# Byte offsets of the moving operands in on-chip memory: FFN activations at byte 32 of 128, token sums at 32, 96 and 64

## The chip, the cores and the metric

The kernel runs on one core of a Trainium2 chip. The metric is the device time of one execution in microseconds (us). Every product is a TensorE matmul: a tile of weights is loaded into the array (LDWEIGHTS, shown as engine PEld) and then the activations stream past it as the moving operand (MATMUL, shown as PE). VectorE is DVE, ScalarE is ACT, GpSimd is POOL, SyncE is SP.

## The reference, cut to what matters

Two blocks of two layers each work on 512 tokens of width 1024 in float32. Six feed-forward networks (FFN) of hidden width 2816 lie in them, and between them projections and attention. What is computed in each FFN:

```python
def swiglu(x, w_gate, w_up, w_down):
    return (jax.nn.silu(x @ w_gate) * (x @ w_up)) @ w_down

def swiglu_ffn(h, w_gate_up, w_down):
    g, u = jnp.split(h @ w_gate_up, 2, axis=-1)
    return (jax.nn.silu(g) * u) @ w_down
```

## The kernel before

**Three products for one.** The kernel keeps a float32 value as a high and a low part of type fp32r. A tile product is three matmuls: high weights by high activations, low weights by high activations, high weights by low activations. Each of them has its own weight load of 128x128. The function `piece` (lines 749 to 751), the functions `chunk_high` and `chunk_low` (757, 758, 761), the early part of the down projection (982 to 984) and the output projections (1388 to 1390) do this with 512 tokens as the moving operand; `product` (899 to 901) does it with 256.

**An FFN has three parts.** First 8 plain pieces of gate and up (24 matmuls of 512 tokens each). Then 9 pairs of hidden chunks: a pair makes four quadrants (gate and up, first and second half of the tokens) from seven products instead of eight, with sums of weights and sums of token halves. A product is 24 matmuls of 256 tokens, a pair 168. Last the down projection, 22 hidden chunks by 8 output chunks, 528 matmuls of 512 tokens or their halves.

**Which tiles the seven products of a pair read** (lines 911 to 926): products 0, 3 and 5 stream the normalised activations HH and HL; product 1 streams the token sum TH[0] and TL[0], product 2 TH[1], product 4 TH[2], product 6 TH[3]. The weights come from the slots that `part_slots` names: (1, 2, 3, 0, 8, 9, 10) for products 0 to 6, or (2, 3, 0, 1, 8, 9, 10) in the two FFNs of the second block.

**Where the tiles lie.** `region` hands out bytes of each partition one after the other; tile sizes are multiples of 32 bytes. The first byte is 16512, a multiple of 128. HH, HL and weight slots 0 to 3 begin at byte 0 of their 128. Behind Y come small tables with 9920 bytes in all, so that the arena `ar` of 88 KB begins at 139072, which is byte 64 of its 128. In the arena lie the hidden activations HIDL and HIDH, the four token sums, the projections, the latents CH and CL, the attention output OH and OL and the normalised memory NH and NL, all at offsets of whole KB, and the weight slots 4 to 8; slots 9 and 10 lie outside at byte 0. A slot holds 8 KB: low weights in the first 4 KB, high weights in the second. Each 128x128 tile in it is 512 bytes further, and a chunk of activations is 1 or 2 KB further, so that all tiles of one buffer have the same byte of their 128. In the table "moving" and "weights" are these bytes:

| matmuls | moving | weights | columns |
|---|---|---|---|
| HH by slots 0 to 3, 9 | 0 | 0 | 512 and 256 |
| HH by slots 4 to 7 | 0 | 64 | 512 |
| HIDH, CH, OH by slots 0 to 3 | 64 | 0 | 512 (a few HIDH: 256) |
| NH by slots 0 to 3 | 64 | 0 | 256 |
| products 1, 2 and 6 | 64 | 0 | 256 |
| product 4 (slot 8) | 64 | 64 | 256 |

**Order around it.** SP issues the weight loads (`load`, `part`), POOL adds weight sums for the pairs (lines 658, 663, 669) or splits plain pieces (629, 631), ACT makes high parts (1697 in pairs, 1718 in the down projection), DVE low parts (2240, 2316), and PE waits for them by semaphores. The order on each engine is written out by hand.

Of the kernel before, what the change touches and what calls it, by code (L numbers as in the profile page):

```python
# [131 lines left out]
def program(nc, A, trips):  # L132
# [5 lines left out]
    def region(n):  # L138
        o = at[0]
        at[0] += n  # L140
        assert at[0] <= nc.sbuf_usable_end, at[0]
        return o

    def sb(name, shape, dt=F32, offset=None):
        n = int(np.prod(shape[1:])) * (2 if dt == BF16 else 4)
        o = region(-(-n // 32) * 32) if offset is None else offset
        return nc.alloc_sbuf_tensor_at(name, list(shape), dt, offset=o)

    KB = 1024
# [4 lines left out]
    slot_at = [region(8 * KB) for _ in range(RING)]  # L154
# [4 lines left out]
    SQo = region(4 * KB)  # L159
# [4 lines left out]
    Yo = region(16 * KB)  # L164
# [11 lines left out]
    stat = sb("stat", [P, 8, 4])  # L176
    top8 = sb("top8", [P, QB, 8])
    WIT = sb("WIT", [P, QB, IDXH], offset=RYo)
    ar = region(88 * KB)
    slot_at += [ar + 72 * KB, ar + 80 * KB, ar + 28 * KB, ar + 36 * KB, ar + 64 * KB, SQo, Yo + 8 * KB]  # L180
    raw = [sb(f"raw{j}", [P, TILES * P], offset=o) for j, o in enumerate(slot_at)]
    WL = [sb(f"WL{j}", [P, TILES * P], F32R, offset=o) for j, o in enumerate(slot_at)]
    WH = [sb(f"WH{j}", [P, TILES * P], F32R, offset=o + 4 * KB) for j, o in enumerate(slot_at)]
# [1 line left out]
    HIDL = sb("HIDL", [P, KF, S], F32R, offset=ar)  # L185
    HIDH = sb("HIDH", [P, KF, S], F32R, offset=ar + KF * 2 * KB)
    BF = sb("BF", [P, KD, S], offset=ar + 8 * KB)
    sum_at = [ar + 48 * KB, ar + 56 * KB, ar + 72 * KB, ar + 80 * KB]
    TF = [sb(f"TF{i}", [P, HALF_K, HALF], offset=o) for i, o in enumerate(sum_at)]
    TL = [sb(f"TL{i}", [P, HALF_K, HALF], F32R, offset=o) for i, o in enumerate(sum_at)]  # L190
    TH = [sb(f"TH{i}", [P, HALF_K, HALF], F32R, offset=o + 4 * KB) for i, o in enumerate(sum_at)]
# [1367 lines left out]
    def _(act):  # L1559
# [443 lines left out]
        for kind in ("dsa", "dil"):  # L2003
# [17 lines left out]
            if kind == "dsa":  # L2021
                act.wait_ge(vt_ready, n.full(vt_ready))
                act.activation(WIT[:], index_weight_bank.rearrange("p (b c) -> p b c", c=P)[:, :, 0:IDXH],
                               ACT.Copy, scale=float(IDXH ** -0.5 * HD ** -0.5)).then_inc(vt_done, 1)
# [25 lines left out]
    def _(dve):  # L2050
# [567 lines left out]
        def logit(i):  # L2618
# [5 lines left out]
            if h == 0:  # L2624
                ins = dve.tensor_scalar(score[b][:], got, WIT[:, b, h:h + 1], None, ALU.mult)
            else:
                ins = dve.scalar_tensor_tensor(out=score[b][:], in0=got, scalar=WIT[:, b, h:h + 1],
                                               in1=score[b][:], op0=ALU.mult, op1=ALU.add)
# [330 lines left out]
def build(nc, arrays, trips):  # L2959
    A = {k: nc.dram_tensor(f"in_{k}", v.shape, mybir.dt.from_np(v.dtype), kind="ExternalInput").ap() for k, v in arrays.items()}  # L2960
    A["out"] = nc.dram_tensor("out_0", (KD, P, S), F32, kind="ExternalOutput").ap()
    program(nc, A, trips)
# [14 lines left out]
```

## Time and profile before

| what | value |
|---|---|
| median of 3 runs | 3335.26 us (3335.03 to 3341.03) |
| span of the profiled execution | 3337.3 us |
| PE busy | 3229.6 us (97%) |
| PEld busy | 2729.8 us (82%) |
| DVE, ACT, POOL busy | 2059.6, 1359.2, 1345.4 us |
| mean granted TensorE clock | 0.993 |

The profiled execution is 2.0 us longer than the median. The time of a matmul in a row of the timeline is its latency (0.28 or 0.39 us), and neighbours overlap. What counts is the distance from the start of one to the start of the next: it is read here as the start of the first matmul of a group of 24 and the start of the first one of the next group, divided by 24.

### The profile page before, as it was taken

The numbers are of one execution on the slowest core, as the hardware profiler recorded it, in microseconds if no ns is written. First come the engines' busy times: TensorE is split into PE (matmuls) and PEld (weight loads), VectorE is DVE, ScalarE is ACT, GpSimd is POOL, SyncE is SP. The second block draws the span as 40 slices with busy tenths as digits, with TensorE's granted clock in tenths as the row PEclk, the third lists the DMA queues.
The fourth block names the chain that finished last, engine by engine and source line by source line (L and its number), as shares of the span: only waits on it lengthen the run. The fifth ranks groups of instructions, "written<-read, shape, count | busy, mean of one in ns | idle before, by whom it ended". The sixth has DMA issues, their size and how long they took to land.

```text
span 3337.3 us, 51827 instructions
## 1 busy us (share of the span) xinstructions
PE 3229.6 (97%) x19480; PEld 2729.8 (82%) x19487; DVE 2059.6 (62%) x2673; ACT 1359.2 (41%) x2335; POOL 1345.4 (40%) x643
## 2 busy tenths in 40 slices
PE   8999999999999999999999999998999999999998
PEld 7998775789877899877579987765789987879986
DVE  7774444586647876354477765678477734477753
ACT  5553225344435445322444543324435521254542
POOL 6320562554116541065164404656553107635300
PEclk9999999999999999999999999999999999999999
DMA  4543221255332454322035533221145433215532
GB/s 156 159 143 104 90 87 32 70 152 151 114 123 83 138 160 120 105 83 87 19 99 153 153 117 108 101 68 34 51 135 166 123 103 108 82 57 146 168 104 95
DMA packets 99977, 362.59 MB, mean 109 GB/s; under 512 B 11088, under 2 KB 11344, under 8 KB 99536
## 3 DMA queue, kind: packets, MB, share of 16 engines
q1 hardware_dynamic: 88704, 320.90, 29.4%
q0 software_dynamic: 7776, 28.32, 5.1%
q10 hardware_dynamic: 3312, 10.86, 0.9%
q8 instruction: 122, 2.00, 0.2%
q14 instruction: 63, 0.52, 0.0%
HBM read 355.84 MB, written 4.19 MB: 108 GB/s over the span
## 4 chain that ended last, share of the span: by engine, by line
PE 73%; DVE 10%; issue 6%; ACT 4%; POOL 3%; DMA 3%; DVEq 0%; ACTq 0%; POOLq 0%; SPq 0%
PE psC L749 4%; PE psC L751 4%; PE psC L750 4%; PE psA L749 4%; PE psA L751 4%; PE psA L750 4%; PE psD L899 2%; PE psD L900 2%; PE psD L901 2%; PE psB L899 2%; PE psB L900 2%; PE psB L901 2%; DVE WL L2240 2%; DMA Y<-in_ws 2%; PE psB L984 2%
## 5 line engine op out<-in xcount | busy, mean ns | idle before, releaser
L629 POOL TENSOR_TENSOR WH<-raw,scalars 128x1024 fp32r<-128x1024 f32 (+1 forms) x194 | 377.8, 1948 | 1206.5 <-DMA raw<-in_w 1143.3
L2240 DVE TENSOR_TENSOR WL<-raw,WH 128x1024 fp32r<-128x1024 f32 x324 | 447.9, 1385 | 70.5 <-POOL raw L663 39.8
L631 POOL TENSOR_TENSOR WL<-raw,WH 128x1024 fp32r<-128x1024 f32 (+1 forms) x194 | 471.2, 2429 | 15.2
L1697 ACT ACTIVATE WH<-raw 128x1024 fp32r<-128x1024 f32 x324 | 340.4, 1053 | 48.9 <-DMA raw<-in_ws 37.2
L2316 DVE TENSOR_TENSOR WL<-raw,WH 128x1024 fp32r<-128x1024 f32 (+1 forms) x144 | 163.1, 1135 | 307.4 <-ACT WH L1718 305.8
L658 POOL TENSOR_TENSOR raw<-raw,Y 128x1024 f32<-128x1024 f32 x54 | 133.4, 2471 | 509.6 <-DMA raw<-in_ws 509.6
L1718 ACT ACTIVATE WH<-raw 128x1024 fp32r<-128x1024 f32 (+1 forms) x144 | 141.9, 989 | 375.7 <-DMA raw<-in_w 375.7
L749 PE MATMUL psA<-HH,WH 128*128 128x512 f32 x560 | 230.0, 411 | 0.0
L751 PE MATMUL psA<-HL,WH 128*128 128x512 f32 x560 | 218.5, 390 | 0.0
L750 PE MATMUL psA<-HH,WL 128*128 128x512 f32 x560 | 218.3, 390 | 0.0
L899 PE MATMUL psD<-TH,WH 128*128 128x256 f32 x720 | 202.0, 281 | 6.2 <-DVE psC L2287 2.7
L900 PE MATMUL psD<-TH,WL 128*128 128x256 f32 x720 | 200.5, 279 | 0.0
L901 PE MATMUL psD<-TL,WH 128*128 128x256 f32 x720 | 200.3, 278 | 0.0
L749 PE MATMUL psC<-HIDH,WH 128*128 128x512 f32 x484 | 191.8, 396 | 3.5 <-DVE WL L2316 3.5
L750 PE MATMUL psC<-HIDH,WL 128*128 128x512 f32 x484 | 191.4, 396 | 0.0
L751 PE MATMUL psC<-HIDL,WH 128*128 128x512 f32 x484 | 191.4, 395 | 0.0
L899 PE MATMUL psB<-TH,WH 128*128 128x256 f32 x576 | 161.9, 281 | 5.1 <-ACT psB L1734 5.1
L669 POOL TENSOR_TENSOR raw<-raw,raw 128x1024 f32<-128x1024 f32 x54 | 142.8, 2645 | 47.3 <-PE psB L901 27.5
L900 PE MATMUL psB<-TH,WL 128*128 128x256 f32 x576 | 160.6, 279 | 0.0
L901 PE MATMUL psB<-TL,WH 128*128 128x256 f32 x576 | 160.4, 278 | 0.0
L899 PEld LDWEIGHTS psD<-TH,WH 128*128 128x128 f32 x720 | 135.9, 189 | 8.3 <-DVE psC L2287 3.5
L663 POOL TENSOR_TENSOR raw<-raw,raw 128x1024 f32<-128x1024 f32 x54 | 134.0, 2482 | 13.4 <-POOL raw L658 11.6
(540 smaller groups left out, 9631.1 us busy)
## 6 DMA issues: line engine op xcount, KB each, us to landing
raw<-in_w SPq DMA_DIRECT2D x338, 512.0 KB, 3.5
raw<-in_ws SPq DMA_DIRECT2D x216, 512.0 KB, 3.6
Y<-in_ws SPq DMA_DIRECT2D x54, 512.0 KB, 4.7
raw<-in_ws POOLq DMA_DIRECT2D x54, 512.0 KB, 5.4
X<-in_x ACTq DMA_DIRECT2D x4, 512.0 KB, 9.5
NRAW<-in_mem ACTq DMA_DIRECT2D x2, 1024.0 KB, 7.2
out<-Y SPq DMA_DIRECT2D x8, 256.0 KB, 2.1
POSI<-in_pos ACTq DMA_DIRECT2D x4, 256.0 KB, 2.6
```

The lines of the kernel that those rows point to most:

```text
L629: pool.tensor_tensor(WH[j][:, 0:w], raw[j][:, 0:w], zero[:, 0:1].broadcast_to([P, w]), ALU.subtract).then_inc(w_hi, 1)
L631: pool.tensor_tensor(WL[j][:, 0:w], raw[j][:, 0:w], WH[j][:, 0:w], ALU.subtract).then_inc(w_split, 1)
L669: pool.tensor_tensor(raw[slots[5]][:], raw[slots[2]][:], raw[slots[3]][:], ALU.add).then_inc(sum_ready, 1)
L749: pe.matmul(out, WH[slot][:, w], hi[:, t], start=start and t == 0, stop=False)
L750: pe.matmul(out, WL[slot][:, w], hi[:, t], start=False, stop=False)
L751: mm = pe.matmul(out, WH[slot][:, w], lo[:, t], start=False, stop=stop and t == tiles - 1)
L899: pe.matmul(o, WH[slot][:, w], hi[:, k], start=start and half == 0 and k == 0, stop=False, skip_group_check=True)
L900: pe.matmul(o, WL[slot][:, w], hi[:, k], start=False, stop=False, skip_group_check=True)
L901: mm = pe.matmul(o, WH[slot][:, w], lo[:, k], start=False, stop=half == 1 and k == HALF_K - 1, skip_group_check=True)
L1697: act.activation(WH[slots[i]][:], DX if i == 6 else raw[slots[i]][:], ACT.Copy).then_inc(part_hi, 1)
L2240: dve.tensor_tensor(WL[slots[i]][:], DX if i == 6 else raw[slots[i]][:], WH[slots[i]][:], ALU.subtract).then_inc(part_lo, 1)
L2316: dve.tensor_tensor(WL[j][:, 0:w], raw[j][:, 0:w], WH[j][:, 0:w], ALU.subtract).then_inc(down_lo, 1)
```

## The change

```diff
     WIT = sb("WIT", [P, QB, IDXH], offset=RYo)
+    region(96)
     ar = region(88 * KB)
-    slot_at += [ar + 72 * KB, ar + 80 * KB, ar + 28 * KB, ar + 36 * KB, ar + 64 * KB, SQo, Yo + 8 * KB]
+    slot_at += [ar + 72 * KB, ar + 80 * KB, ar + 28 * KB, ar + 36 * KB, ar + 64 * KB - 160, SQo, Yo + 8 * KB]
...
-    sum_at = [ar + 48 * KB, ar + 56 * KB, ar + 72 * KB, ar + 80 * KB]
+    sum_at = [ar + 48 * KB - 256, ar + 56 * KB - 192, ar + 72 * KB - 96, ar + 80 * KB - 96]
```

The arena moves up by 96 bytes, from byte 64 to byte 32 of its 128. With it move HIDL, HIDH, the projections, CH, CL, OH, OL, NH, NL and the weight slots 4 to 7. The token sums are placed by themselves: TH[0] at byte 32, TH[1] at 96, TH[2] and TH[3] at 64, where the last two were. Slot 8, which holds the weights of product 4, goes from byte 64 to byte 0. No instruction, wait, transfer or size is added, removed or moved.

| matmuls | moving, weights before | after |
|---|---|---|
| HIDH, CH, OH (512 columns), NH (256) | 64, 0 | 32, 0 |
| HH by slots 4 to 7 | 0, 64 | 0, 32 |
| product 1 | 64, 0 | 32, 0 |
| product 2 | 64, 0 | 96, 0 |
| product 4 | 64, 64 | 64, 0 |
| product 6 | 64, 0 | 64, 0 |
| HH by slots 0 to 3, 9 | 0, 0 | 0, 0 |

## Rows read from the trace of the kernel before

**Rows 1.** The page: span, busy time of each engine, TensorE's clock in 40 slices.

```profile
span 3337.3 us, 51827 instructions
PE 3229.6 (97%) x19480; PEld 2729.8 (82%) x19487; DVE 2059.6 (62%) x2673; ACT 1359.2 (41%) x2335; POOL 1345.4 (40%) x643
PEclk9999999999999999999999999999999999999999
```

**Rows 2.** Stretches: two pairs, one disturbed pair, down projection. Busy us (instructions), clock, DMA.

```profile
102.68:122.33 19.65, 19.65 (x171) 19.65 (x169) 14.09 (x18) 9.23 (x15) 8.03 (x4) 1.00 0.57 161
122.33:141.98 19.65, 19.65 (x171) 19.65 (x170) 14.65 (x18) 10.12 (x15) 8.22 (x6) 1.00 0.57 162
1829.90:1850.70 20.80, 19.98 (x170) 19.79 (x169) 15.15 (x19) 9.84 (x14) 9.69 (x5) 1.00 0.52 151
335.00:346.20 11.20, 11.20 (x50) 9.02 (x49) 3.05 (x3) 3.09 (x4) 0.00 (x0) 1.00 0.32 95
```

**Rows 3.** Timeline of PE, first matmul of products 0 to 6, then next pair.

```profile
102.68 0.28 PE L899 MATMUL psC<-HH,WH 128*128 128x256 f32 x1
105.54 0.29 PE L899 MATMUL psC<-TH,WH 128*128 128x256 f32 x1
108.28 0.28 PE L899 MATMUL psD<-TH,WH 128*128 128x256 f32 x1
111.00 0.28 PE L899 MATMUL psC<-HH,WH 128*128 128x256 f32 x1
113.86 0.28 PE L899 MATMUL psD<-TH,WH 128*128 128x256 f32 x1
116.72 0.28 PE L899 MATMUL psD<-HH,WH 128*128 128x256 f32 x1
119.59 0.29 PE L899 MATMUL psD<-TH,WH 128*128 128x256 f32 x1
122.33 0.28 PE L899 MATMUL psA<-HH,WH 128*128 128x256 f32 x1
```

**Rows 4.** Timeline of PE, hidden by slots 0 to 3: firsts of three pieces of 24.

```profile
335.40 0.39 PE L749 MATMUL psC<-HIDH,WH 128*128 128x512 f32 x1
...
341.00 0.39 PE L749 MATMUL psC<-HIDH,WH 128*128 128x512 f32 x1
...
346.60 0.39 PE L749 MATMUL psC<-HIDH,WH 128*128 128x512 f32 x1
```

**Rows 5.** Timeline of PE: HH by slot 1 (2442.36), by slot 6 (2447.80), next piece.

```profile
2442.36 0.39 PE L749 MATMUL psC<-HH,WH 128*128 128x512 f32 x1
...
2447.80 0.39 PE L749 MATMUL psA<-HH,WH 128*128 128x512 f32 x1
...
2453.30 0.39 PE L749 MATMUL psB<-HH,WH 128*128 128x512 f32 x1
```

**Rows 6.** Timeline of PE: attention output OHa, 24 matmuls between its two rows.

```profile
2406.32 0.39 PE L1388 MATMUL psC<-OHa,WH 128*128 128x512 f32 x1
...
2411.93 0.39 PE L1388 MATMUL psC<-OHa,WH 128*128 128x512 f32 x1
```

**Rows 7.** Timeline of PE: normalised memory NH, 24 matmuls between its two rows.

```profile
2258.11 0.28 PE L749 MATMUL psA<-NH,WH 128*128 128x256 f32 x1
...
2260.93 0.28 PE L749 MATMUL psA<-NH,WH 128*128 128x256 f32 x1
```

**Rows 8.** Groups of PE instructions: count | busy us, mean ns | idle before, by whom.

```profile
L749 PE MATMUL psC<-HIDH,WH 128*128 128x512 f32 x484 | 191.8, 396 | 3.5 <-DVE WL L2316 3.5
L982 PE MATMUL psB<-HIDH,WH 128*128 128x512 f32 x264 | 104.4, 396 | 0.0
L982 PE MATMUL psA<-HIDH,WH 128*128 128x512 f32 x264 | 104.4, 395 | 0.0
L749 PE MATMUL psC<-CH,WH 128*128 128x512 f32 x68 | 28.3, 416 | 1.9 <-DVE PROJ L2406 1.9
L1388 PE MATMUL psC<-OHa,WH 128*128 128x512 f32 x64 | 25.4, 397 | 0.0
L1388 PE MATMUL psC<-OHb,WH 128*128 128x512 f32 x32 | 12.8, 399 | 0.0
```

**Rows 9.** Waits: who waited for whom, us in total, times, longest.

```profile
POOL raw L658 <- DMA raw<-in_ws: 509.6, 48, 13.2
ACT WH L1718 <- DMA raw<-in_w: 375.7, 114, 6.3
DVE WL L2316 <- ACT WH L1718: 305.8, 98, 6.0
```

## The prediction

> **What bounds the kernel now.** The page comes first: PE is busy 3229.6 of 3337.3 us, and no other engine passes 62% but the weight loads, which run beside PE [rows 1]. Such a share alone proves little, since a share is a mean, so the second view is the stretches: in an undisturbed pair and in the down projection PE is busy in all of the time, at a granted clock of 1.00, which is the 2.4 GHz level [rows 2]. So the end is set by how quickly one matmul follows another, and the third view is the timeline, read for distances between starts. There the reader is to see that matmuls of one size don't all follow at one distance, and what goes with the difference. In one pair the seven products of 24 matmuls of 256 columns last 2.86, 2.74, 2.72, 2.86, 2.86, 2.87 and 2.74 us [rows 3]. The products that stream HH (0, 3, 5) and product 4 take 2.86: in these four the moving operand and the weights begin at the same byte of their 128. The products whose activations begin at 64 and whose weights at 0 (1, 2, 6) take 2.72 to 2.74. Settled, that is 120 ns for equal bytes (2.86/24 is 119.2; the first few of a product are shorter) and 113 to 114 ns for 64 apart. Product 4 shows that it isn't the tile: it streams a token sum as product 6 does, into the same bank, and costs what HH costs.
>
> With 512 columns it is the other way round. Equal bytes take 5.44/24 = 226.7 ns, HH at 0 with weights at 64 5.50/24 = 229.2 [rows 5], and hidden activations at 64 with weights at 0 5.60/24 = 233.3 [rows 4]; the attention output, in the same position, 5.61/24 = 233.8 [rows 6]. The memory rows, 256 columns, activations at 64 and weights at 0, take 2.82/24 = 117.5 [rows 7], and not 113: the same bytes can settle at two distances, and which one depends on how the stretch is entered. 15 of the 108 products 1 and 2 have 118, 1 of the 54 products 6.
>
> **The change part by part.** Nothing is added or removed; every cost is a count times a change of distance. PE is full where these matmuls lie, so a saved nanosecond is a nanosecond of the end unless a wait takes it.
>
> *Product 4, equal bytes to 64 apart.* It becomes what product 6 is, behind a product that streams HH, as product 6 is. 54 of them (six FFNs, nine pairs): 2.86 to 2.74 is 0.12 us, by the unrounded medians 2.855 and 2.739, so 54 x 0.116 = 6.3 us less. If it settled at 118 always, 2.82 [rows 7], only 54 x 0.03 = 1.6 less. I take 6.3, since only 5 of the 108 products 1 and 6, which also follow HH, are at 118.
>
> *512 columns, activations 64 to 32.* Hidden: 3 x 484 + 6 x 264 = 3036; latents 3 x 68 and attention output 3 x 96 are 492 more [rows 8]; 3528 together. No row has 32, so it needs bounds. Below: a matmul of 256 columns is 106.7 ns shorter than one of 512 with the same bytes (226.7 against 120), so the best 256-column distance, 113.3, stands for 220.0 with 512; that is 13.3 less than now, 47 us. Above: the hidden matmuls alternate between 231 and 236 ns, and a settled 236 would be 2.7 more, 9.5 us. Of the three positions with 512 columns two lie at 226.7 and 229.2 and only the one that is now left lies at 233.3. I take the mean of those two, 227.9, as nearest: 5.4 x 3528 = 19 us less.
>
> *Products 1 and 2, 64 to 32 and to 96.* 108 products, now at 2.74 and 2.72. Above: what equal bytes cost, 2.86, which is 54 x 0.12 + 54 x 0.14 = 14 us more. Below: by the same amount the other way, 14 less, for nothing in the rows says that 64 is the best place. If the cost rises from 64 towards 0 on both sides, both lose half of it, 7 us; if it falls steadily round the 128 bytes, 32 and 96 lie on opposite sides of 64 and cancel. I take the middle of these, 3.5 more.
>
> *The rest.* HH by slots 4 to 7 (624 matmuls: 3 pieces in four FFNs, 2 in two, 2 at each of five borders, 24 each) goes from 64 apart to 32 apart, between 226.7 and 233.3 where it now has 229.2: 1.6 less to 2.6 more. 264 hidden matmuls of 256 columns and 192 of NH lie between 113 and 120: 1 less to 2 more. Both taken at nothing. The elementwise work is as long on any of the slots, and it has slack: in the down projection ACT waits 376 us for weights to land and DVE 306 us for ACT [rows 9], and both are busy 3.1 of 11.2 us there [rows 2], so PE at 228 ns is still fed. If that cover were gone the 19 us would turn into waits on L2316. In the pairs POOL waits 510 us for transfers [rows 9] and is busy 8 of 19.65 us [rows 2]; but a few pairs already hold PE up (19.98 busy of 20.80 [rows 2]), and in these a faster product 4 gives nothing: at most a quarter of the 6.3.
>
> Sum: -6.3 - 19 + 3.5 = -22 us. The profiled execution is 2.0 us longer than the median, 3335.3, from which I subtract: 3313 us.
>
> The Trainium skill, page "SBUF — State Buffer", section "Who interferes with whom", has a rule that speaks against any effect: TensorE has two independent read ports, one for the moving operand and one for weight loads, and "PE and ACT never wait on anyone". By it the sum would be 0. The trace doesn't agree: product 4 and product 6 differ by 0.12 us in 2.86 though only the bytes differ.
>
> **The rivals.**
> *It does nothing.* The position doesn't matter, and the differences come from the order of the products. Against it: product 4 against 6, and HH by slot 1 against slot 6. 3335 us. The page named above would have it so.
> *32 acts like 64 for the wide ones.* Only product 4 changes: 3335.3 - 6.3 = 3329 us. For it: rows only tell 0 and 64 apart, and a coarse grain is possible; against it, a 64-byte grain would put 32 with 0, which gives the forecast.
> *32 is better than either.* 512 columns fall to 220.0: -47 - 6.3 and 0 to -14 for products 1 and 2, 3268 to 3282 us. For it: in 256 columns the distance of 64 gains 6.7 ns on equal bytes, and nothing says that 226.7 is the floor of the wide ones. The Trainium skill, page "TensorE: Matmul & The Clock Gate", section "Back-to-back issue gap", gives N/2.4 + 2.5 ns, 215.8 for 512 columns; by it the wide ones would save 17.5 x 3528 = 62 us; no row here is that short.
> *Slower: 32 collides longer than 64.* Weight load and moving stream meet for longer: wide ones settle at 236 (+9.5) and products 1 and 2 at the price of equal bytes (+14), less 6.3: +17, 3352 us. For it: 256 columns are now at their best position, and two of the three TH products leave it. It decides once these two terms together pass 6.3 + 6.7 = 13 us.
>
> **How the numbers follow.** A measurement of this kernel can tell about 0.2%, 6.7 us, from no change. Chances: the forecast (wide ones between 226.7 and 230) 0.55; 32 better than either 0.15; 32 acts like 64 0.13; nothing 0.02; slower 0.15. The time is the first one's, 3313. The range leaves out the far half of "better than either" and of "slower": 3280 to 3344. Faster by over 0.2%: 0.55 + 0.15 + a little of the 3329 case, 0.72; within 0.2%: 0.15; slower: 0.13, since some of the slower case stays under 6.7 us.
>
> **What would show it.** Product 4 at 2.74 us; 24 hidden matmuls at 5.44 to 5.50 us instead of 5.60; the same for OHa; products 1 and 2 at 2.68 to 2.80; products 0, 3, 5 and 6 and HH by slots 0 to 3 as before. A down projection with gaps ahead of PE would show that weights had become the bound. The prediction is wrong if 24 hidden matmuls take 5.60 or more, or under 5.35.

## The result

| kernel | median us | against before |
|---|---|---|
| before | 3335.05 (3329.60 to 3341.03, 5 runs) | |
| after | 3347.20 (3344.61 to 3349.41, 5 runs) | 1.0035 (95% interval 1.0025 to 1.0046) |

The change makes the kernel 12 us slower (8 to 15 by the interval). The forecast was 3313 us, with a range from 3280 to 3344. The head of the page of after, to be read beside [rows 1]:

```profile
span 3343.4 us, 51827 instructions
PE 3238.1 (97%) x19480; PEld 2739.2 (82%) x19487; DVE 2060.3 (62%) x2673; ACT 1359.3 (41%) x2335; POOL 1341.2 (40%) x643
PEclk9999999999999999999999999999999999999999
```

The same instructions, PE still full, the clock as before, and no other engine busier by more than 1 us: PE has 8.5 us more, and the weight loads that run beside it 9.4. So the time is looked for again in the distance between matmuls. The timeline of PE in after shows the first matmul of products 0 to 6 of the same pair, and of the next pair (lines are one further down than in [rows 3]):

```profile
102.89 0.28 PE L900 MATMUL psC<-HH,WH 128*128 128x256 f32 x1
105.75 0.28 PE L900 MATMUL psC<-TH,WH 128*128 128x256 f32 x1
108.59 0.28 PE L900 MATMUL psD<-TH,WH 128*128 128x256 f32 x1
111.46 0.28 PE L900 MATMUL psC<-HH,WH 128*128 128x256 f32 x1
114.33 0.28 PE L900 MATMUL psD<-TH,WH 128*128 128x256 f32 x1
117.16 0.28 PE L900 MATMUL psD<-HH,WH 128*128 128x256 f32 x1
120.03 0.29 PE L900 MATMUL psD<-TH,WH 128*128 128x256 f32 x1
122.77 0.28 PE L900 MATMUL psA<-HH,WH 128*128 128x256 f32 x1
```

The pair lasts 19.88 us instead of 19.65. By the medians over all pairs, product 1 went from 2.739 to 2.833 us, product 2 from 2.720 to 2.870, product 4 from 2.855 to 2.822, product 3, whose bytes are as before but which follows product 2, from 2.862 to 2.878; products 0, 5 and 6 are as they were. That is 0.23 us for a pair, 12 us for 54.

The down projection, the 24 matmuls between two firsts as in [rows 4], and below them HH by slot 6 between its two firsts, as in [rows 5]:

```profile
325.30 0.40 PE L750 MATMUL psC<-HIDH,WH 128*128 128x512 f32 x1
...
330.90 0.40 PE L750 MATMUL psC<-HIDH,WH 128*128 128x512 f32 x1
...
2450.17 0.39 PE L750 MATMUL psA<-HH,WH 128*128 128x512 f32 x1
...
2455.76 0.40 PE L750 MATMUL psB<-HH,WH 128*128 128x512 f32 x1
```

The hidden matmuls take 5.60 us for 24, to the hundredth what they took. The 19 us that the forecast expected from them aren't there. HH by slots 4 to 7 went the wrong way, from 5.50 to 5.59 us for 24: 624 matmuls at 233.4 instead of 229.1 ns (both read where they have settled), 2.7 us more. The hidden matmuls of 256 columns, in the timelines of before and then of after, 24 between two rows:

```profile
348.00 0.28 PE L1016 MATMUL psB<-HIDH,WH 128*128 128x256 f32 x1
...
350.73 0.28 PE L1016 MATMUL psC<-HIDH,WH 128*128 128x256 f32 x1
```

```profile
349.80 0.28 PE L1017 MATMUL psB<-HIDH,WH 128*128 128x256 f32 x1
...
352.61 0.28 PE L1017 MATMUL psC<-HIDH,WH 128*128 128x256 f32 x1
```

2.73 to 2.81 us for 24, on 264 matmuls: 0.8 us more. The terms add to 12.4 + 2.7 + 0.8 = 16 us, four more than the medians differ. The two profiled executions differ by only 6.1 us in span. The idle time of PE ahead of the products accounts for about what lies between 16 and 6.1. This is the view of line 900 in after, idle time in us and how often, by what ended it; in before, line 899, the first three of these rows are 14.2, 14.0 and 9.9 us, and all idle time there is 46.8 us against 35.4 here, 11.4 less.

```profile
  issue: 12.5, 17
  DVE WL L2241: 9.5, 16
  ACT psB L1735: 7.3, 12
  DVE psC L2288: 6.1, 8
```

That a slower PE gives the weights more time and so shortens the waits would fit, but one execution of each is too little to show it. Apart from the first two pairs of each FFN, 4 pairs last over 0.5 us longer than the steady one in the profiled execution of before, and none in after.

### The profile page after: what moved, and what is told of

It is laid out like the page before. It is cut to its first block, busy times and chain, and to the rows that moved or that the text cites. A ratio compares the mean times of both kernels' runs of the same rounds, so it can differ in the third digit from the quotient of the medians.

```text
span 3343.4 us, 51827 instructions
## 1 busy us (share of the span) xinstructions
PE 3238.1 (97%) x19480; PEld 2739.2 (82%) x19487; DVE 2060.3 (62%) x2673; ACT 1359.3 (41%) x2335; POOL 1341.2 (40%) x643
## 4 chain that ended last, share of the span: by engine, by line
PE 79%; DVE 9%; issue 5%; ACT 4%; POOL 2%; DMA 1%; DVEq 0%; ACTq 0%; SPq 0%; POOLq 0%
PE psC L750 4%; PE psC L752 4%; PE psC L751 4%; PE psA L750 4%; PE psA L752 4%; PE psA L751 4%; PE psD L902 3%; PE psD L900 3%; PE psD L901 3%; PE psB L900 3%; PE psB L902 3%; PE psB L901 3%; PE psC L902 2%; PE psC L900 2%; PE psC L901 2%
## 5 line engine op out<-in xcount | busy, mean ns | idle before, releaser
L2241 DVE TENSOR_TENSOR WL<-raw,WH 128x1024 fp32r<-128x1024 f32 x324 | 450.3, 1393 | 58.1 <-ACT WH L1698 29.2
```

The costliest lines, as they stand in the source:

```text
L2241: dve.tensor_tensor(WL[slots[i]][:], DX if i == 6 else raw[slots[i]][:], WH[slots[i]][:], ALU.subtract).then_inc(part_lo, 1)
```

## The experiments

Bytes are told from here on modulo 256, for a reason that the third experiment gives. In before the arena begins at 64 of 256, HH and the slots outside the arena at 128. In after the arena is at 160, the four sums at 160, 224, 64 and 64, and slot 8 at 0. "Difference" is the byte of the moving operand less that of the weights, modulo 256.

### The arena alone (e1)

```diff
+    region(96)
     ar = region(88 * KB)
...
-... ar + 64 * KB, SQo, Yo + 8 * KB]
+... ar + 64 * KB - 96, SQo, Yo + 8 * KB]
...
-    sum_at = [ar + 48 * KB, ar + 56 * KB, ar + 72 * KB, ar + 80 * KB]
+    sum_at = [ar + 48 * KB - 96, ar + 56 * KB - 96, ar + 72 * KB - 96, ar + 80 * KB - 96]
```

> Only the arena moves to byte 32 of 128; the four token sums and slot 8 stay at byte 64, as before. The theory (position theory: the distance from one matmul to the next is set by the bytes of moving operand and weights, and for 512 columns 32 costs what 64 costs) expects 24 hidden matmuls at 5.60 us, a steady pair at 19.65 us as before, the hidden matmuls of 256 columns at 118 instead of 113 ns, and a time within 3 us of before. The rival, that the move of the arena itself costs (weights land in slots 4 to 7 at another byte, other engines write to another byte), expects most of the 12 us here.

Measured: 3334.29 us, ratio 1.0001 (0.9988 to 1.0013). 24 hidden matmuls take 5.60 us and the seven products what they took in before, with a steady pair of 19.65. The interval is 4 us either way, and the 3.5 us of the HH pieces and of the narrow hidden matmuls are inside it. The arena's move, with everything that DMA and the other engines write at new bytes, is not what costs the 12 us.

### The two sums alone (e2)

```diff
-    sum_at = [ar + 48 * KB, ar + 56 * KB, ar + 72 * KB, ar + 80 * KB]
+    sum_at = [ar + 48 * KB - 160, ar + 56 * KB - 96, ar + 72 * KB, ar + 80 * KB]
```

> Only the first two token sums move, to bytes 32 and 96; arena, slot 8 and the other sums as before. The position theory expects product 1 to go from 2.74 to 2.83 us and product 2 from 2.72 to 2.87, a steady pair of 19.65 + 0.09 + 0.15 + 0.02 = 19.91 us, over 54 pairs 14 us: about 3349. The rival (move of the arena costs) expects a time within 2 us of before.

Measured: 3348.36 us, ratio 1.0044 (1.0027 to 1.0061), 15 us more, 9 to 20 by the interval: as much as the whole change, as far as the two intervals tell. Products 1 and 2 between their firsts and that of product 3, timeline of PE in this kernel:

```profile
106.04 0.28 PE L899 MATMUL psC<-TH,WH 128*128 128x256 f32 x1
108.87 0.28 PE L899 MATMUL psD<-TH,WH 128*128 128x256 f32 x1
111.74 0.28 PE L899 MATMUL psC<-HH,WH 128*128 128x256 f32 x1
```

2.83 and 2.87 us, as in after. The steady pair is 19.91 us, as expected. These two experiments settle where the 12 us came from: the place of the two sums.

### Slot 8 alone (e3)

```diff
-    ar = region(88 * KB)
-... ar + 64 * KB, SQo, Yo + 8 * KB]
+    ar = region(88 * KB + 128)
+... ar + 64 * KB + 64, SQo, Yo + 8 * KB]
...
-    sum_at = [ar + 48 * KB, ar + 56 * KB, ar + 72 * KB, ar + 80 * KB]
+    sum_at = [ar + 48 * KB, ar + 56 * KB, ar + 72 * KB + 128, ar + 80 * KB + 128]
```

> Slot 8 moves from byte 64 to byte 0, the third and fourth sums move by 128 bytes and so keep byte 64 of 128; the rest as before. Product 4 was 2.86 us before and is 2.82 in the changed kernel (118 ns settled), though product 6, with the same bytes of 128, is 2.74 (113 ns). Three theories. Only bytes of 128 count and product 4 was held at 118 by what ran before it (product 2 at byte 96, then product 3): product 4 at 2.74, product 6 at 2.74, pair 19.53, 6 us less. Bytes of 256 count (moving less weights is 64 of 256 for product 4 in the changed kernel and 192 for product 6): here both are 64 of 256, so both 2.82, pair 19.70, 2 to 3 us more. Something of slot 8 or of the third sum by itself: product 4 2.82, product 6 2.74, pair 19.62, 2 us less.

Measured: 3339.50 us, ratio 1.0019 (1.0008 to 1.0029). Timeline of PE in this kernel, firsts of products 4, 5 and 6 and of the next pair:

```profile
114.50 0.28 PE L899 MATMUL psD<-TH,WH 128*128 128x256 f32 x1
117.33 0.29 PE L899 MATMUL psD<-HH,WH 128*128 128x256 f32 x1
120.22 0.28 PE L899 MATMUL psD<-TH,WH 128*128 128x256 f32 x1
123.05 0.29 PE L899 MATMUL psA<-HH,WH 128*128 128x256 f32 x1
```

Products 4 and 6 both take 2.83 us, in all 54 pairs settled at 118 ns. Product 6 has the same bytes of 128 as in before, where it took 2.74: only its sum has moved by 128. So positions 128 bytes apart aren't the same, and a theory in bytes of 128 is too coarse. Of the three theories put down, bytes of 256 stands. The products that follow 4 and 6 begin some 0.01 to 0.02 us worse (2.883 for products 5 and 0 by the medians), so that the pair is 19.75 and not 19.70.

### The arena at the weights' byte (e4)

```diff
+    region(64)
     ar = region(88 * KB)
...
-... ar + 64 * KB, SQo, Yo + 8 * KB]
+... ar + 64 * KB - 128, SQo, Yo + 8 * KB]
...
-    sum_at = [ar + 48 * KB, ar + 56 * KB, ar + 72 * KB, ar + 80 * KB]
+    sum_at = [ar + 48 * KB - 192, ar + 56 * KB - 192, ar + 72 * KB - 64, ar + 80 * KB - 64]
```

> The arena begins at byte 0, so that the hidden, latent and attention matmuls of 512 columns have equal bytes, as HH by slots 0 to 3; the four sums stay at byte 64 and slot 8 is at byte 0. Position theory: 24 hidden matmuls go from 5.60 to 5.44 us, 3528 x 6.6 ns = 23 us less, hidden matmuls of 256 columns from 113 to 120 (2 us more), HH by slots 4 to 7 from 229 to 227 (1.5 less), product 4 at 2.74 (6 us less) or 2.82 (2 less): 3335 - 29 = 3306 or 3310. If bytes of 256 count, products 1, 2 and 4 are all at 64 of 256 and take 2.82: 10 us worse, 3318. If the wide matmuls' distance comes from the tile (hidden) and not from its byte, 5.60 stays and the time is near 3330.

Measured: 3323.53 us, ratio 0.9961 (0.9940 to 0.9982). Timeline of PE, 24 hidden matmuls, then 24 of HH by slot 6:

```profile
325.47 0.39 PE L750 MATMUL psC<-HIDH,WH 128*128 128x512 f32 x1
...
330.91 0.39 PE L750 MATMUL psC<-HIDH,WH 128*128 128x512 f32 x1
...
2440.70 0.39 PE L750 MATMUL psA<-HH,WH 128*128 128x512 f32 x1
...
2446.14 0.39 PE L750 MATMUL psB<-HH,WH 128*128 128x512 f32 x1
```

5.44 us in both: the gain that the forecast had looked for at byte 32 is there with both operands at 128 of 256. Products 1, 2 and 4 have the difference 64 here and settled at 118 ns in 53, 53 and 54 of 54 pairs (medians 2.831, 2.827, 2.822 us), and product 6, with 192, at 113 in all. That is what bytes of 256 say, and the steady pair is 19.83 us. The time is 5 us above the 3318 of that case; that case stood for 17 us less than before, and the interval allows 6 to 20.

### A map of the differences (e5 and e6)

The first half:

```diff
+    region(160)
     ar = region(88 * KB)
-... ar + 28 * KB, ar + 36 * KB, ar + 64 * KB, SQo, Yo + 8 * KB]
+... ar + 28 * KB + 32, ar + 36 * KB + 64, ar + 64 * KB - 192, SQo, Yo + 8 * KB]
...
-    sum_at = [ar + 48 * KB, ar + 56 * KB, ar + 72 * KB, ar + 80 * KB]
+    sum_at = [ar + 48 * KB - 224, ar + 56 * KB - 192, ar + 72 * KB - 64, ar + 80 * KB - 64]
```

> A map of distances by the byte of the moving operand less the byte of the weights, taken modulo 256. The theory so far: that difference sets the distance, with 0: 120 ns, 192: 113, 64: 118, 32: 118, 96: 120 for 256 columns, and 0: 227, 64: 229, 192: 233, 32: 233 for 512. Here product 1 has 128, product 2 160, product 4 128, product 6 32; hidden 96; HH by slots 4 and 5 160, by slot 6 128, by slot 7 96. If bytes of 128 were what counts, product 1 and product 4 (0 of 128) take 120, product 2 (32) 118, hidden 233 or less. If bytes of 256 count, product 6 is at 118 and the others are open between 113 and 120, the wide ones between 227 and 233.

The second half:

```diff
+    region(32)
-    ar = region(88 * KB)
-    slot_at += [ar + 72 * KB, ar + 80 * KB, ar + 28 * KB, ar + 36 * KB, ...
+    ar = region(88 * KB + 128)
+    slot_at += [ar + 72 * KB, ar + 80 * KB + 64, ar + 28 * KB + 32, ar + 36 * KB + 128, ...
...
-    sum_at = [ar + 48 * KB, ar + 56 * KB, ar + 72 * KB, ar + 80 * KB]
+    sum_at = [ar + 48 * KB, ar + 56 * KB, ar + 72 * KB + 128, ar + 80 * KB + 128]
```

> Second half of the map: products 1 and 2 have the difference 224 of 256, product 4 128, product 6 96; hidden 224; HH by slot 4 32, by slot 5 224, by slot 6 0, by slot 7 160. The theory (difference modulo 256) expects product 4 as in the first half of the map, product 6 at 120, HH by slot 4 at 233 as hidden at 32, HH by slot 6 at 227, and HH by slot 5 at the value of hidden. If a buffer's own address counted and not the difference, HH by slot 4 would differ from hidden at 32.

One execution of each, 3348.5 and 3348.7 us; what counts is the timeline. With the kernels above, and with those of the last section for 256 columns, the settled distances in ns; behind them the bytes of 256 at which each was seen, moving operand by weights:

| difference | 256 columns (a product, us) | bytes | 512 columns | bytes |
|---|---|---|---|---|
| 0 | 120 (2.86) | 128 by 128, 64 by 64 | 226.7 | 128 by 128 |
| 32 | 117 to 118 (2.83) | 160 by 128 | 233 | 160 by 128, 128 by 96 |
| 64 | 118 (2.82 to 2.83) | 64 by 0, 192 by 128 | 229 | 128 by 64 |
| 96 | 120 (2.87 to 2.88) | 224 by 128 | 233 | 224 by 128, 128 by 32 |
| 128 | 119 (2.85) | 0 by 128, 160 by 32, 224 by 96 | 233 | 128 by 0 |
| 160 | 117 (2.82) | 32 by 128 | 234 | 128 by 224 |
| 192 | 113 (2.72 to 2.74), or 118 (2.82) | 64 by 128, 192 by 0; 128 by 192 | 233 | 64 by 128 |
| 224 | 118 (2.84) | 96 by 128 | 233 | 96 by 128, 128 by 160 |

For 512 columns the differences 0, 64, 128, 160 and 192 were each seen at one pair of bytes alone, so that there the difference and the bytes themselves are not told apart.

With a slot moved to the moving operand's byte, its matmuls fall to 227: HH by slot 6 in the second half (difference 0) and in the first half (128), each 24 matmuls up to the row that follows:

```profile
53.32 0.39 PE L750 MATMUL psB<-HH,WH 128*128 128x512 f32 x1
...
58.77 1.02 PE L770 MATMUL psD<-cf 128*128 128x512 f32 x2
```

```profile
53.25 0.40 PE L750 MATMUL psB<-HH,WH 128*128 128x512 f32 x1
...
58.84 1.02 PE L770 MATMUL psD<-cf 128*128 128x512 f32 x2
```

5.45 against 5.59 us. For 512 columns one difference is good (0), one is fair (64), and the other six are alike. For 256 columns one is good (192) and the other seven lie between 117 and 120. Both expectations held where they named a number, to about 1 ns.

### Every product at its best difference (e7 and e8)

```diff
+    region(64)
     SQo = region(4 * KB)
...
-... ar + 64 * KB, SQo, Yo + 8 * KB]
+... ar + 72 * KB, SQo, Yo + 8 * KB]
...
-    sum_at = [ar + 48 * KB, ar + 56 * KB, ar + 72 * KB, ar + 80 * KB]
+    sum_at = [ar + 48 * KB - 64, ar + 56 * KB - 64, ar + 64 * KB - 64, ar + 80 * KB]
```

> Every wide matmul of the arena at difference 0 and products 1, 2, 4, 5 and 6 at 192 of 256 (SQ, T and Y move by 64 bytes, so slots 9 and 10 and the arena with them; the third sum and slot 8 change places). The theory expects products 4 and 5 at 2.74 us, products 1, 2 and 6 as before, a pair of 19.65 - 0.12 - 0.13 = 19.40 us or 14 us less over 54 pairs, 24 hidden matmuls at 5.44 us (23 us less), hidden of 256 columns at 120 (2 more), HH by slots 4 to 7 at 227 (1.5 less): 3333 - 36 = 3297. The rival is that POOL's chain of sums, which now ends ahead of PE in a pair, takes over at 19.65 us: then 3311. A second rival: with differences 64 instead of 192 for product 5, because the weights and not the activations were moved, product 5 takes 2.82 and the sum is 5 us smaller.

Measured: 3316.14 us, ratio 0.9939 (0.9924 to 0.9954). Hidden at 5.44 us and product 4 at 2.74 as expected, but products 5 and 6 take 2.82 and 2.83, though their difference is 192. The pair is 19.59 us and not 19.40, which is 10 us over 54 pairs; with these, 3308 would have been expected instead of 3297, and the measured time is 8 us above that. What the two products have in common is that their weights begin at 192, in slots 9 and 10.

The next kernel keeps those two slots as they were:

```diff
+    region(64)
     ar = region(88 * KB)
...
-... ar + 64 * KB, SQo, Yo + 8 * KB]
+... ar + 80 * KB, SQo, Yo + 8 * KB]
...
-    sum_at = [ar + 48 * KB, ar + 56 * KB, ar + 72 * KB, ar + 80 * KB]
+    sum_at = [ar + 48 * KB - 64, ar + 56 * KB - 64, ar + 64 * KB - 64, ar + 72 * KB - 64]
```

> The arena begins at byte 0 of 128 (128 of 256), as the weights; all four sums begin at 64 of 256 and slot 8 at 128, the pairing that gave 113 ns in every run so far; slots 9 and 10 as before. Bytes of moving operand and weights are now (64, 128) of 256 for products 1, 2, 4, 6 and (128, 128) for all the rest. Expected: products 1, 2, 4, 6 at 2.72 to 2.74 us, products 0, 3, 5 at 2.86, a steady pair of 19.65 - 0.12 = 19.53 us, against 19.59 with e7; hidden at 5.44 us; 3527 matmuls x 6.6 ns = 23 us less, 6 less from product 4, 1.5 less from HH by slots 4 to 7, 2 more from hidden of 256 columns: 3334 - 28 = 3306. The rival (the chain of sums and splits, which already held up some pairs, takes what product 4 gives): pairs with gaps ahead of PE, and 3312.

Measured: 3315.24 us, ratio 0.9941 (0.9928 to 0.9953): 17 us under the before measured beside it (16 to 24 us by the interval), where after lies 12 above its own, with nothing changed but addresses. Timeline of PE in this kernel, firsts of the products 3 to 6 and of the next pair, in a pair without waits:

```profile
760.43 0.28 PE L900 MATMUL psA<-HH,WH 128*128 128x256 f32 x1
763.29 0.29 PE L900 MATMUL psB<-TH,WH 128*128 128x256 f32 x1
766.03 0.28 PE L900 MATMUL psB<-HH,WH 128*128 128x256 f32 x1
768.89 0.29 PE L900 MATMUL psB<-TH,WH 128*128 128x256 f32 x1
771.63 0.28 PE L900 MATMUL psC<-HH,WH 128*128 128x256 f32 x1
```

All steady distances are what was expected, the pair at 19.52 us. The time is 9 us above 3306, and the 28 us less that were expected lie outside the interval. The idle time of PE ahead of line 900 in this kernel (its profiled execution is the longest of its six, 3323 us):

```profile
  DVE WL L2241: 19.4, 37
  issue: 14.9, 20
  ACT psB L1735: 10.6, 15
  DVE psC L2288: 9.8, 11
  ACT psD L1735: 3.4, 5
```

58.1 us in all against 46.8 in before, the wait for low weights up from 14.0 to 19.4 us in 37 places instead of 23. The chain of waits in such a stretch of this kernel runs through the weights, a round in 20.87 us (1784.59 to 1805.46):

```profile
1784.59 1.24 DVE WL L2241
1786.00 6.09 DMA Y<-in_ws
1792.12 1.24 issue
1793.45 2.37 POOL raw L659
1796.14 2.38 POOL raw L664
```

With a transfer of 6.1 us the round of the weight sums is longer than PE's 19.52. It is longer than the 19.65 of before too, and before has such pairs (20.80 us in [rows 2]): apart from the first two pairs of each FFN, 7 pairs last over 0.5 us longer than the steady one in this execution, 4 in that of before. In such a pair a faster product 4 gives nothing. That is the rival put down for this run. That it took a part of the gain fits these rows; how large a part was not tried alone, and one execution of each doesn't tell whether the faster PE made such pairs more frequent: e9 below, with slower pairs than before, has 9 of them, and e10, with pairs like those of before, none.

### Difference or address (e9 and e10)

```diff
-... ar + 64 * KB, SQo, Yo + 8 * KB]
+... ar + 72 * KB - 64, SQo, Yo + 8 * KB]
...
-    sum_at = [ar + 48 * KB, ar + 56 * KB, ar + 72 * KB, ar + 80 * KB]
+    sum_at = [ar + 48 * KB - 128, ar + 56 * KB - 128, ar + 64 * KB - 128, ar + 80 * KB]
```

> The arena as before; product 4 reads its sum at 192 of 256 and its weights at 0, products 1 and 2 their sums at 192 and weights at 128, product 6 as before at 64 and 128. If the difference modulo 256 sets the distance, product 4 (192) takes 2.74 us, products 1 and 2 (64) 2.82. If both addresses matter and only 64 by 128 gives 113 ns, product 4 stays at 2.82 like products 5 and 6 of e7, which had the difference 192 with other bytes and settled at 118.

Measured, one execution (3347.1 us): product 4, moving operand at 192 and weights at 0, takes 2.736 us and settled at 113 ns in all 54 pairs; products 1 and 2, at the difference 64, 2.831 and 2.827. So 64 by 128 isn't the only good pairing.

```diff
-... ar + 64 * KB, SQo, Yo + 8 * KB]
+... ar + 72 * KB - 128, SQo, Yo + 8 * KB]
...
-    sum_at = [ar + 48 * KB, ar + 56 * KB, ar + 72 * KB, ar + 80 * KB]
+    sum_at = [ar + 48 * KB - 256, ar + 56 * KB - 256, ar + 64 * KB - 192, ar + 80 * KB]
```

> Product 4 reads its sum at 128 of 256 and its weights at 192, the bytes at which products 5 and 6 of e7 settled at 118 ns though their difference is 192; products 1 and 2 are at 64 and 128 as before, the arena too. If the weights' own byte matters beside the difference, product 4 takes 2.82 us here; if the difference alone matters and e7's two products were held at 118 by what ran ahead of them (product 4 at 113 ahead of product 5), product 4 follows product 3 with equal bytes as in e8 and takes 2.74.

Measured, one execution (3334.0 us): product 4, at 128 with weights at 192, takes 2.829 us and settled at 118 ns in all 54 pairs, behind a product 3 with the same bytes as in e8, where product 4 settled at 113 in all 54. So the difference alone isn't enough: in a product that follows without a gap, the difference 192 gave 113 ns with the weights at 0 or 128 of 256, and 118 with the weights at 192.

Weights at 192 don't rule out the 113 ns, though. In e7, product 6 follows product 5 without a gap in 49 pairs, and all 49 settled at 118. In the other five, each the first pair of an FFN, a gap lay just ahead of it, and three of these settled at 113. Timeline of PE in e7, the first matmul of such a product 6, and two firsts of threes further on with 12 matmuls from one to the other:

```profile
703.46 0.39 PE L900 MATMUL psD<-TH,WH 128*128 128x256 f32 x1 [0.82 <-DVE psC L2288]
...
704.61 0.28 PE L900 MATMUL psD<-TH,WH 128*128 128x256 f32 x1
...
705.97 0.28 PE L900 MATMUL psD<-TH,WH 128*128 128x256 f32 x1
```

1.36 us for 12 is 113.3 ns, at the bytes 128 by 192. In before it is the same the other way round: product 2, at 64 by 128, settled at 113 in all 37 pairs in which it began without a gap, and the 11 pairs at 118 are among the 17 in which a gap lay at its start. So at this difference both distances are open, with the weights at 128 and at 192 alike, and which of them a product settles at depends on how it is entered; with no gap ahead of it, the bytes of the product itself have a part in that. The difference 64 isn't tied to 118 either: in e4 and e9, 7 of its 270 products settled at 113. Why it is so, no run shows.

## Why the prediction was wrong

**What bounds the kernel** held: with the same instructions, the time went the way of the distances in every kernel, and the slack of the down projection was there as told: with 24 hidden matmuls in 5.44 us, PE's idle time ahead of them rose only from 3.5 us in before to between 5.5 and 5.7 us in e4, e7 and e8. In the pairs some of the gain of e7 and e8 is missing, and waits like those of [rows 2] are the likely place.

**512 columns, 64 to 32** is the step that failed, and it carried the forecast: 19 us less, measured nothing, in e1 as in after; 24 hidden matmuls took the 5.60 us that the prediction had named as the sign of being wrong. It took the mean of two other positions as the value of a third that no row had, on the ground that 64 was the outlier. The map shows the reverse: 233 ns is what six of eight differences cost, and 227 and 229 are the exceptions. The rows already held the warning. HH by slot 6 and hidden by slots 0 to 3 are both 64 of 128 apart, and they differ, 229 against 233 [rows 4, 5]. The text took them as two positions in an asymmetric list. Had it taken the disagreement seriously, it would have asked for a second variable, and modulo 256 the two are at differences 64 and 192. The rival "32 acts like 64 for the wide ones" was right on this term, at a chance of 0.13. This step is half of the miss: with the wide ones at nothing the sum would have been 3 us less, still with the wrong sign, and the terms below are the other half.

**Products 1 and 2**: 3.5 us more expected, with an upper bound of 14. Measured 0.094 + 0.150 us, in 54 pairs 13.2 us more, nearly the bound. The rows' best position was given up for two unknown ones, and the value was put near the middle between the bounds, 14 less and 14 more. The map shows 117 to 120 ns at seven of eight differences, so that 113 was the exception and nearly every move away from it costs.

**Product 4**: 6.3 us less expected, measured 54 x 0.033 = 1.8, the other end that the text had named (1.6). The ground for the choice was that product 6 has the same bytes behind the same kind of product. The same bytes of 128, but not of 256: a difference of 64 against 192 (e3, e9). The counts behind the choice are one too high, which changes nothing: 14 of the 108 products 1 and 2 settled at 118 and not 15, and 4 of the 108 products 1 and 6, not 5.

**HH by slots 4 to 7** was taken at nothing with 2.6 us as its upper end, and measured 2.7, since it left the fair difference. The narrow hidden matmuls cost 0.8 within their bounds. Product 3, at 0.016 us a pair 0.9 us, was not foreseen: its bytes are as before, and it changed with the product ahead of it.

**The rival that came true** is "slower", 3352 us at 0.15, with half of its mechanism: products 1 and 2 near the price of equal bytes, but the wide ones unmoved and not at 236. With these two taken from the runs, -1.8 + 13.2 + 2.7 + 0.8 + 0.9 = 16 us more, and the median moved by 12.

**Two independent read ports** are what the Trainium skill, page "SBUF — State Buffer", section "Who interferes with whom", gives TensorE, one for the moving operand and one for weight loads, with the rule "PE and ACT never wait on anyone"; of addresses it says nothing. The runs don't agree that the two are independent: HH at one and the same byte takes 229.1 ns by slots 4 to 7 in before and 233.4 in after, where only the weights have moved against it, and in e2 the move of two sums costs 15 us (9 to 20). **The gap of N/2.4 + 2.5 ns**, 215.8 and 109.2 ns, which the Trainium skill, page "TensorE: Matmul & The Clock Gate", section "Back-to-back issue gap", gives for a single matmul by itself, was reached by none of the positions tried: the shortest settled distances were 226.7 and 113.3. For a stream of weight loads and matmuls of 512 columns the same section has about 131 ns, and no stretch here comes near it.

## What to carry to other kernels

Where PE is full and loads new weights for every matmul, read the distance between starts by pairs of buffers, and compare the addresses of the moving operand and the weights modulo 256; for 512 columns in fp32r both at the same byte was best here (seen at 128 of 256 alone), for 256 columns the moving operand 192 further than weights that begin at 0 or 128. Read afterwards what each product settled at, since the one ahead of it and a gap ahead of it count too. If two rows that should agree by your rule don't, the rule lacks a variable; and a term that rests on a value no row has should be taken at what most rows cost. Before giving up a position that is the best seen, try the new one on a single buffer.

## What was not expected of the hardware

The distance between matmuls depends on addresses, and positions 128 bytes apart are not the same (e3), while all of the map fits a period of 256: 226.7 to 234 ns with 512 columns, 113 to 120 with 256, at a granted clock of 1.00 in the stretches read, the 2.4 GHz level. The best difference for one width (0 for 512) is one of the worst for the other (120 ns for 256). A position can have two settled distances: at the difference 192 with weights at 128, product 2 had 113 ns in 43 and 118 in 11 of 54 pairs of before, and all 11 are among the 17 with a gap at its start. The memory rows have the same bytes, and settled at 118 in before [rows 7]. One kernel of this study (e8), with no instruction changed, gains 17 us of 3332.
